# RWKV scan: the mask of the next subchunk taken earlier, the block substitution moved ahead of the levels, and its DMAs spread over three queues

## The reference, cut to what matters

```
def step(S, inp):
    r_t, w_t, k_t, v_t, kk_t, b_t = inp
    sa = jnp.einsum('bhij,bhj->bhi', S, -kk_t)
    S = (S * w_t[:, :, None, :] + sa[..., None] * b_t[:, :, None, :]
         + v_t[..., None] * k_t[:, :, None, :])
    return S, jnp.einsum('bhij,bhj->bhi', S, r_t)
...
y = (rwkv7_scan(r_h, heads(decay[:, :, 0]), k_h, v_h, kk, b_h, False)
     + rwkv7_scan(r_h, heads(decay[:, :, 1]), k_h, v_h, kk, b_h, True))
```

## Time and profile before

| | |
|---|---|
| median of 3 runs | 3489.02 us |
| the profiled execution | 3487.46 us |
| its span | 3486.2 us |
| the scan in the span | about 700 to 1083 us |
| start of one transposed copy to the next, 14 of them from 748.12 to 1061.85 us | 22.4 us mean |
| PE busy in such a stretch | 19.5 us without `cum`, 21.2 to 21.5 us with it |
| DVE busy in such a stretch | about 18.4 us |
| granted TensorE clock in the steady scan | 1.00 |

### The profile page before, as it was taken

One profiled execution on the slowest core, in us unless ns is written; L12 is line 12 of the kernel. 1 busy time (PEld: TensorE's weight loads), 2 busy tenths in 40 slices (PEclk: granted clock), 3 DMA queues, 4 the chain that ended last, 5 costly groups with the idle time before them and its releaser, 6 DMA issues.

```text
span 3486.2 us, 58522 instructions
## 1 busy us (share of the span) xinstructions
PE 3188.2 (91%) x25755; PEld 2622.4 (75%) x25755; DVE 2211.3 (63%) x2948; ACT 971.9 (28%) x1514; POOL 469.5 (13%) x373
## 2 busy tenths in 40 slices
PE   6988788979987999999999897998998799999996
PEld 4777767778885878888888676875667688888885
DVE  5758655778887444444444575997556566666666
ACT  4544233312113221111111444112663111111112
POOL 2530023423224000000000121000001011111110
PEclk9979788989998999999999998999999899999999
DMA  4410044322224011111111202114001111111111
GB/s 131 122 66 14 16 142 138 111 45 42 37 36 166 19 55 51 40 55 53 38 55 43 91 31 74 49 43 99 2 2 61 43 49 49 49 49 49 49 49 67
DMA packets 242726, 207.27 MB, mean 59 GB/s; under 512 B 66744, under 2 KB 205255, under 8 KB 241959
## 3 DMA queue, kind: packets, MB, share of 16 engines
q1 hardware_dynamic: 223527, 176.82, 17.1%
q10 hardware_dynamic: 13824, 25.17, 2.2%
q0 software_dynamic: 5120, 1.53, 0.5%
HBM read 171.93 MB, written 29.64 MB: 58 GB/s over the span
## 4 chain that ended last, share of the span: by engine, by line
PE 70%; DVE 17%; ACT 5%; POOL 2%; issue 2%; DMA 2%; SPq 1%; ACTq 0%; DVEq 0%; POOLq 0%
PE ps L2169 23%; PE ps L2184 17%; PE ps L2031 5%; PE ps L636 3%; PE ps L637 3%; PE ps L638 3%; DVE Yc L2794 2%; DVE s_tmp L1662 2%; DVE s_Z L1663 2%; PE ps L2893 2%; PE ps L2921 1%; PE ps L2911 1%; PE ps L1480 1%; POOL a_x L2544 1%; PE ps L1008 1%
## 5 line engine op out<-in xcount | busy, mean ns | idle before, releaser
L3198 DVE TENSOR_TENSOR H<-H,ps 128x1024 f32<-128x1024 f32 x256 | 312.7, 1221 | 181.6 <-PE ps L2184 174.8
L2334 DVE TENSOR_TENSOR fsum<-fsum,ps 128x1024 f32<-128x1024 f32 x168 | 205.2, 1221 | 312.4 <-PE ps L2184 310.3
L2184 PE MATMUL ps<-dh,hh 128*128 128x512 f32 x864 | 340.0, 393 | 19.9 <-DVE hl L2149 13.9
L2184 PE MATMUL ps<-dl,hh 128*128 128x512 f32 x864 | 338.7, 392 | 0.0
L2184 PE MATMUL ps<-dh,hl 128*128 128x512 f32 x864 | 338.6, 392 | 0.0
L2169 PE MATMUL ps<-hn_h,uh 128*128 128x512 f32 x704 | 275.8, 392 | 7.2 <-DVE ul L1779 4.7
L2169 PE MATMUL ps<-hn_l,uh 128*128 128x512 f32 x704 | 275.4, 391 | 0.0
L2169 PE MATMUL ps<-hn_h,ul 128*128 128x512 f32 x704 | 275.3, 391 | 0.0
L2169 PE MATMUL ps<-hx_h,uh 128*128 128x512 f32 x512 | 200.9, 392 | 8.4 <-DVE hx_l L2149 5.3
L2184 PEld LDWEIGHTS ps<-dh,hh 128*128 128x128 f32 x864 | 163.8, 190 | 58.0 <-DVE hl L2149 15.6
L2169 PE MATMUL ps<-hx_l,uh 128*128 128x512 f32 x512 | 200.4, 391 | 0.0
(11 more groups left out here) (473 smaller groups left out, 7345.8 us busy)
## 6 DMA issues: line engine op xcount, KB each, us to landing
aw<-in_w_ada_dram ACTq DMA_DIRECT2D x96, 256.0 KB, 2.9
uw<-in_w_mlp_dram SPq DMA_DIRECT2D x32, 512.0 KB, 4.3
dw<-in_w_mlp_dram SPq DMA_DIRECT2D x32, 512.0 KB, 5.2
uw<-in_ffn_gate_dram SPq DMA_DIRECT2D x22, 512.0 KB, 4.0
uw<-in_ffn_up_dram SPq DMA_DIRECT2D x22, 512.0 KB, 5.3
dw<-in_ffn_down_dram SPq DMA_DIRECT2D x22, 512.0 KB, 5.9
cw<-in_w_in_dram SPq DMA_DIRECT2D x20, 512.0 KB, 3.8
o_w<-in_w_out_dram SPq DMA_DIRECT2D x16, 512.0 KB, 9.9
```

What stands on the lines that cost most here:

```text
L2184: mm = pe.e.matmul(ps[:, 2 * pair + hf, :], v[s][:, blk(t)], w[:, half(hf)], start=(m == 0), stop=(m == 2))
L2334: return dve.c.tensor_tensor(f, f, new, ALU.add) if g else dve.c.tensor_copy(f, new)
L3198: return dve.c.tensor_tensor(h, h, self.ps[:, 4 + 2 * (t % 2):6 + 2 * (t % 2), :], ALU.add)
```

## The change

The mask `nm` of subchunk n + 1 is taken at the end of pass u, one pass earlier than before, right after `xt`. `s_N16` and `s_Z16` exist twice, and the transposed copy has a tile of its own, `s_X16`. The substitution's steps 0 to 8 now stand ahead of `t4`, its steps 9 to 14 behind the early mask. `products(u + 3)` is cut in three: the first part stands between `t4` and `zz`, the other two between `t5` and `xt`; `pr` is still on the last. The 16 block loads go over three queues: SP 8, ACT 4, POOL 4. The write to `zd` is two DMAs, both issued by ACT, one for each copy. The identity is copied into `s_Z16` by ACT instead of POOL. ACT's exponentials stand in the following odd pass instead of at the end of the even one.

```diff
 SP, for each n:
-            if n:
-                sp.wait_ge(self.t_z["out", n - 1], self.pool["zero"])
-                self.inverse_back(sp, self.t_z, n - 1, range(0, 8, 2))
-            sp.wait_ge(self.t_n["out", n])
-            self.blocks_there(sp, self.t_n, n, range(0, 5))
+            sp.wait_ge(self.t_no["out", n])
+            self.blocks_there(sp, self.t_n, n, range(0, 4))
+            if n:
+                back(n - 1)
...
-            sp.wait_ge(dve["x16", n])
-            sp.e.dma_start(zd[n % 2]..., self.Z16[:]...).then_inc(*self.t_z.one("out", n))
 ACT:
+            if u % 2 and (u + 3) // 2 < NBLK:
+                self.exps_act((u + 3) // 2)
+            if u >= 0:
+                if u + 2 < NSUB:
+                    act.wait_ge(self.t_zo["out", u])
+                    act.e.activation(self.Z16[u % 2][:], self.eye16[:], ACTF.Copy).then_inc(*act.one("one", u + 2))
                 for d in range(2):
                     act.wait_ge(pe["uu", u, d])
                     act.e.activation(self.U[:, L[d]], self.hb(d, 2, 256), ACTF.Copy).then_inc(*act.one("U", u, d))
+            if 0 <= u + 1 < NSUB:
+                act.wait_ge(self.t_no["out", u + 2] if u + 2 < NSUB else dve["z16", u + 1])
+                if u + 2 < NSUB:
+                    self.blocks_there(act, self.t_na, u + 2, range(4, 6))
+                act.wait_ge(dve["z16", u + 1])
+                act.e.dma_start(zd[1], self.Z16[(u + 1) % 2]...).then_inc(*self.t_zo.one())
+                act.wait_ge(dve["x16", u + 1])
+                act.e.dma_start(zd[0], self.X16...).then_inc(*self.t_zo.one("out", u + 1))
 POOL, for each n:
+            if n < NSUB:
+                pool.wait_ge(self.t_no["out", n])
+                self.blocks_there(pool, self.t_nb, n, range(6, 8))
             if n:
                 ...
                 self.inverse_back(pool, self.t_zb, n - 1, range(1, 8, 2))
-            if n < NSUB:
-                pool.e.tensor_copy(self.Z16[:, :, 1], self.eye16[:]).then_inc(*pool.one("one", n))
-                pool.wait_ge(self.t_n["out", n])
-                self.blocks_there(pool, self.t_nb, n, range(5, 8))
 DVE, pass u:
             if n < NSUB:
-                for w, to, name in ((0, self.NM[n % 3], "nm"), (1, self.MM[n % 3], "mm")):
-                    ...
+                masked(1, n)
...
-            if u + 3 < NSUB:
-                products(u + 3)
+            if n < NSUB:
+                self.substitute_dve(n, 0, 9)
             (t4)
+            if u + 3 < NSUB:
+                products(u + 3, 0)
             (zz, t5)
-            if n < NSUB:
-                self.substitute_dve(n, 0, 4)
+            if u + 3 < NSUB:
+                products(u + 3, 1)
+            if u + 3 < NSUB:
+                products(u + 3, 2)
             (xt)
+            if n + 1 < NSUB:
+                masked(0, n + 1)
             if n < NSUB:
-                self.substitute_dve(n, 4, 15)
+                self.substitute_dve(n, 9, 15)
```

More of the change, by code:

```diff
@@ L412, in plan_block1 @@
         self.room = self.r0 + 184 * 1024
-        self.BKT, self.ZZ2, self.Z16 = [sb("s_BKT", [PART, LANES, 2, CH]) for k in range(3)], sb("s_ZZ2", [PART, LANES, 2, CH]), sb("s_Z16", [32, 2, 2, 16, 16])
+        self.BKT, self.ZZ2, self.Z16 = [sb("s_BKT", [PART, LANES, 2, CH]) for k in range(3)], sb("s_ZZ2", [PART, LANES, 2, CH]), [sb("s_Z16", [32, 2, 16, 16]) for k in range(2)]
         self.room = self.r0 + 16 * 1024
@@ L1441, in sig, with back @@
             sp.e.dma_start(self.sig[:], sg[:, t].rearrange("d p c -> p d c")).then_inc(*self.t_in.one("sig", t))
+        def back(n):
+            sp.wait_ge(self.t_zo["out", n], self.pool["zero"])
+            self.inverse_back(sp, self.t_z, n, range(0, 8, 2))
         sig(1)
@@ L1606, in rwkv_scan_act @@
         L = [slice(0, 4), slice(4, 8)]
+        act.wait_ge(self.t_misc["r_const"])
+        for n in range(2):
+            act.e.activation(self.Z16[n][:], self.eye16[:], ACTF.Copy).then_inc(*act.one("one", n))
         for u in range(-2, NSUB):
@@ L1614, in rwkv_scan_act @@
                     act.e.activation(self.U[:, L[d]], self.hb(d, 2, 256), ACTF.Copy).then_inc(*act.one("U", u, d))
+            if 0 <= u + 1 < NSUB:
+                zd = self.dram["zd"][(u + 1) % 2].rearrange("k x d w i c -> w (k x) d (i c)")
+                act.wait_ge(self.t_no["out", u + 2] if u + 2 < NSUB else dve["z16", u + 1])
+                if u + 2 < NSUB:
+                    self.blocks_there(act, self.t_na, u + 2, range(4, 6))
+                act.wait_ge(dve["z16", u + 1])
+                act.e.dma_start(zd[1], self.Z16[(u + 1) % 2][:].rearrange("p d i c -> p d (i c)")).then_inc(*self.t_zo.one())
+                act.wait_ge(dve["x16", u + 1])
+                act.e.dma_start(zd[0], self.X16[:].rearrange("p d i c -> p d (i c)")).then_inc(*self.t_zo.one("out", u + 1))
+            elif u == -2:
+                act.wait_ge(self.t_no["out", 0])
+                self.blocks_there(act, self.t_na, 0, range(4, 6))
             if 0 <= u < NSUB // 2:
@@ L1662, in substitute_dve @@
             dve.c.tensor_tensor(part, col, pivot, ALU.mult).then_inc(*dve.one())
-            dve.c.tensor_tensor(rows, rows, part, ALU.subtract).then_inc(*dve.one())
+            dve.c.tensor_tensor(rows, rows, part, ALU.subtract).then_inc(*(dve.one("z16", n) if s == 14 else dve.one()))
         if end == 15:
-            dve.c.tensor_copy(self.Z16[:, :, 0], self.Z16[:, :, 1].rearrange("p d i c -> p d c i")).then_inc(*dve.one("x16", n))
+            if n:
+                dve.wait_ge(self.t_zo["out", n - 1])
+            dve.c.tensor_copy(self.X16[:], self.Z16[n % 2][:].rearrange("p d i c -> p d c i")).then_inc(*dve.one("x16", n))
     def rwkv_scan_dve(self):
@@ L1677, in both, with products @@
             return bass.AP(tensor=x.tensor, offset=x.offset, ap=[x.ap[0], [y.offset - x.offset, 2]] + list(x.ap[1:]))
-        def products(n):
+        def products(n, part):
             t, AR, BK, F = n // 2, self.AR[n % 3], self.BK, self.F[n % 3]
@@ L1699, in products @@
[L1699 to L1704, removed]
+            if part == 0:
+                dve.wait_ge(act["Ei", t, 0], act["Ei", t, 1])
+                if n >= 3:
+                    dve.wait_ge(pe["yy", n - 3, 1])
+                if n:
+                    dve.wait_ge(pe["tr", n - 1, 1])
+                dve.c.tensor_tensor(lanes(F[:]), lanes(self.last[:]), end, ALU.mult).then_inc(*dve.one())
+                dve.e.tensor_tensor(lanes(AR[:, :, 0]), both(self.kk[:, :, W], self.kk[:, :, W_b]), Ex, ALU.mult).then_inc(*dve.one())
+            elif part == 1:
+                dve.e.tensor_tensor(lanes(BK[:, :, 0]), both(self.bb[:, :, W], self.bb[:, :, W_b]), En, ALU.mult).then_inc(*dve.one())
+                dve.e.tensor_tensor(lanes(AR[:, :, 1]), both(rkv[:, 0:4, W], rkv[:, 0:4, W_b]), Ei, ALU.mult).then_inc(*dve.one())
+            else:
+                dve.e.tensor_tensor(lanes(BK[:, :, 1]), both(rkv[:, 4:8, W], rkv[:, 4:8, W_b]), En, ALU.mult).then_inc(*dve.one())
+                dve.c.tensor_copy(lanes(self.last[:]), end).then_inc(*dve.one("pr", n))
@@ new lines, in masked @@
+        def masked(w, n):
+            to, name = ((self.NM[n % 3], "nm"), (self.MM[n % 3], "mm"))[w]
+            for d in range(2):
+                dve.wait_ge(pe[("gb", "gk")[w], n, d])
+                dve.e.tensor_tensor(to[:, L[d]].rearrange("p l a b -> p l (a b)"), self.fb(d, w),
+                                    rep(self.gram_mask[:, d].rearrange("p a b -> p (a b)"), 4), ALU.mult).then_inc(*dve.one(name, n, d))
+        for part in range(3):
+            products(0, part)
+        masked(0, 0)
```

33 lines of the change are left out of this document (12 added, 21 removed).

## The result

| | before | after |
|---|---|---|
| median of 10 runs, us | 3489.4 | 3501.4 |
| lowest to highest | 3484.5 to 3499.8 | 3495.1 to 3511.2 |
| ratio after to before | | 1.0037 (95%: 1.0022 to 1.0052) |
| the profiled execution | 3487.5 | 3511.2 |

The changed kernel is slower by 12 us; 3497 was forecast. The profiled execution of the changed kernel happens to be its slowest. So I profiled both kernels twice (experiments 1 and 9) and read the scan by its own marks: start is from the first AR product to the first `t4`, steady from there to the fifteenth `t4`, end from there to the last one.

The account below looks back on a forecast made before the run. Two loops of nearly equal length bound the scan: DVE and DRAM 22.4 us, PE alone 22.1. Terms +1.2 +4.2 +6.8 -4.1 = +8.1 on 3487.5 give 3495.6, plus 1.6 for the median: 3497; own range 3492 to 3501, whole 3484 to 3508.

Parts of the forecast that it names:

- the waits that it named: In the scan: PE idle about 1.6 us ahead of the grams, DVE 1 to 2 us for block loads, none for `nm`.
- Products behind `t5`: DVE's products after `t5` delay the next grams from 0.57 to 2.15 us; PE stands 1.6 us longer in 14 full periods.
- The blocks over three queues: Blocks reach DVE 8.0 us after the mask, DVE waits 1.6; second `zd` write 1.0 us after the copy.
- The copy without POOL: With the identity copy on ACT, the product that took 1.02 us beside POOL's copy takes 0.6.
- The sum of a period: Eight full periods without `cum` take 22.55 us (+0.15 each), six with `cum` 23.1 (+0.7 each).
- The levels: The stretch from `t4` to the end of the second `t5`: 4.5 us in every period.
- The start: Scan's start: uncovered `products(1)` and slow first grams put the first `t4` at 741.3 against 734.49, +6.8 us.
- The end: Pass 13 has no further products, gram or mask; `t4` comes 13.0 us after `t5` instead of 17.1, -4.1 us.
- The first rival: Load paths are shorter than read and PE alone decides the period: not slower, 3485.5 us; chance 0.18.
- The second rival: Queues get in each other's way, so blocks or ZZ come 1 us later: +10 us, 3507; chance 0.25.
- The rule beside it: GpSimd can't write descriptors during a DVE copy within SBUF: blocks 0.6 us later in 8 periods, sum 3502.

Follow-up runs that it names:

- experiment 1: The changed kernel run again unaltered, with a second profile: median 3505.7 us, ratio 1.0033 to the kernel before.
- experiment 9: The kernel before run again unaltered, for a second profile: median 3495.5 us, ratio 0.9998, steady part 321.0 us.
- Experiment 3: Changed kernel, but the grams `gb` wait for the third product instead of the mark `pr` behind the fourth: 3491.7 us, ratio 0.9994 to the kernel before.
- experiment 7: Changed kernel, but block loads read the previous subchunk's buffer and don't wait for the write (result wrong): 3496.8 us, ratio 1.0003 to the kernel before.
- experiment 8: Changed kernel, but block loads over two queues, ten on SP and six on POOL, none on ACT: 3523.7 us, ratio 1.0074 to the kernel before.
- experiment 2: Changed kernel, but `products(1)` stands ahead of the substitution of subchunk 0: 3499.6 us, ratio 1.0007 to the kernel before.
- experiment 4: Changed kernel, but the 512 KB `sig` load waits for `t5` of the subchunk whose ZZ was loaded: 3503.8 us, ratio 1.0023 to the kernel before.
- experiment 10: Changed kernel with `products(1)` early, `gb` waiting for the third product, and 8 double-size block loads instead of 16: 3480.5 us, ratio 0.9950 to the kernel before.
- experiment 11: Changed kernel with `products(1)` early, AR products before the substitution, first BK product between `t4` and `zz`, 8 double block loads: 3480.8 us, ratio 0.9959 to before.

## Why the prediction was right or wrong

The sign held, and so did the waits that it named. The median of 3501.4 lies just above the forecast's own range (3492 to 3501) and inside the whole one (3484 to 3508). The likeliest class did not hold: 0.52 stood on no measurable change, 0.36 on slower, and it is slower. By its own steps:

*Products behind `t5`*: right. PE's grams start 2.07 after `t5` (2.15 forecast), after 1.33 of idle. Experiment 3 takes 0.8 of it away and gets 0.8 in the quiet periods with `cum` and 0.4 to 0.9 in those without. Those without `cum` gain too, because the mask, the write and the block loads hang on the grams as well. That was in my own chain; the sum's wording put the cost on PE's periods alone.

*The blocks over three queues*: the path was 7.5 where read (8.0), and it does end periods, by experiments 7 and 8. That ACT's place in it costs the `zd` write 0.9 us is seen (1.0 forecast).

*The copy without POOL*: right. The products take 0.60 each, the 1.02 of the earlier trace rows is gone.

*The sum of a period* failed in its size, in both directions. Quiet periods are shorter than forecast, 22.7 and 21.8 to 22.2 against 23.1 and 22.55. But each of the two profiles has seven of 23.3 to 24.9. Without the levels the forecast's periods sum to 256.0 (6 x 18.6 and 8 x 18.05), and 257.7 and 255.4 were measured: right in the sum, by short and long ones that cancel. I had summed fixed durations. Four things in a row now have no slack behind them: the write to `nd`, the block loads, the write to `zd`, the ZZ loads. Any one that is late adds its lateness.

*The levels* are the term that was mis-sized. I took 4.5 us for them in every period. In the changed kernel they took 5.4 to 6.2 in five and in three of the 14 periods of the two profiles, and in one of the two ends, at a granted clock below 0.8. Against the kernel before that is +3.1 in the steady part and +0.7 in the end, together as much as the 3.6 between the forecast's 8.1 and the 11.7 measured. 1.6 of it, in both profiles, is the first stretch of levels, right behind the 9 us for which PE stands at the start. In the full periods the slow ones follow waits of PE of 1.5 to 3.8 us, but waits of 1.2 to 2.0 were followed by no slow one in the first profile of the kernel before, and one of 2.8 by none in the second of the changed kernel; so how long PE stood doesn't alone decide it, and the cause stays open. The kernel before has it as well: I took one profile of it as its fixed time, and only experiment 9 showed its steady part to be 3.6 below the mean of two.

*The start*: +6.8 as forecast, and experiment 2 shows that the products and the grams behind them are the cause. To the tenth it is luck. The slow first grams are there (3.32 us for 32), but steps 0 to 8 ended 39.4 after the first products instead of 41.0, and the first `t4` then waited 2.2 us, which the forecast did not have, for the ZZ load behind the sig load (experiment 4).

*The end*: -3.0 where -4.1 was forecast. The second profile's 17.8 us is as forecast (17.6); in the first (19.4) the levels ahead of the last copy took 5.9 us instead of 4.5, with a granted clock of 0.79 from 1074 to 1082.

*The first rival* (PE alone decides) is out. Waits of DVE for blocks run through all profiles of the changed kernel. *The second rival* has its part in single periods, by late ZZ loads and by POOL's late start; its sum of +10 on top of the forecast is not there.

*The rule beside it.* The rule of the Trainium skill (SBUF — State Buffer, section "SBUF: two separate sides") would have POOL's issues stretched by the copy of 0.6 us that now falls among them. The traces agree, but only where the copy hits the beginning of an issue:
```profile
806.29 2.87 POOL L1426 DMA_DIRECT2D s_N<-nd_dram  x4 [15.06 <-DMA nd_dram<-s_NM]
806.57 0.59 DVE L1686 COPY s_X<-s_Z 32x512 f32<-32x512 f32 x1
...
876.88 2.48 POOL L1426 DMA_DIRECT2D s_N<-nd_dram  x4 [15.50 <-DMA nd_dram<-s_NM]
877.28 0.59 DVE L1686 COPY s_X<-s_Z 32x512 f32<-32x512 f32 x1
```
In the first pass the copy began 0.28 us after POOL's first issue, and that issue took 1.02 instead of 0.62; in the second it began 0.40 after, and none was longer. Over the eleven profiles of the changed kernel and of its variants every block load's issue that the copy met from 0.1 before to 0.28 after its start took 0.69 us or more and ended 0.15 us (0.26 in experiments 10 and 11) behind the copy; every one that it met from 0.30 on kept its time. In the changed kernel that is three passes of 14 in one profile and one in the other, 0.1 to 0.4 us each, instead of 0.6 in 8 periods.

What stays open: why POOL starts its block loads 1.4 us later at subchunks 8 and 15, what makes the granted clock fall in one pass and not in another, and why the last ZZ load lands some 1 us late in some passes in which no sig load is near.

## What to carry to other kernels

Before work is moved to "behind" a step, look at which mark sits on its last instruction and who waits for that mark: here three products with the mark on the small copy behind the last cost PE 1.3 us in every pass, and moving the mark alone won as much as the whole change lost. In a pipelined loop a prologue pass runs the same code without the cover that the steady passes have, so it is to be priced by itself. And a loop whose slack has been taken out pays for every late DMA: compare such versions with two profiles each, inside the stage, and against the spread of the kernel before. Sum apart the stretches of fixed work whose length hangs on the clock: without the levels, the profiles of the changed kernel and of experiments 2 and 4 agree within 3 us, with them only within 5.

## What the runs showed of the hardware

The issue of a small DMA cost by the piece hardly at all: 0.62 us for 64 pieces of 64 bytes on POOL, 0.70 for 128; 0.37 per load on ACT and SP. A POOL issue whose beginning a DVE copy within SBUF met took up to 1.03 us instead of 0.62 and ended 0.15 us behind the copy. A ZZ load of 16 KB that POOL issued 0.12 to 0.26 us behind SP's sig load of 512 KB took 4.0 to 5.2 us to land in most cases, and 2.0 where the sig load came later. A POOL copy beside a DVE product with both inputs in SBUF lengthened the product from 0.60 to 1.02 us, and the product is back at 0.60 with the copy on ACT. After PE had waited some 3.8 us its granted clock was 0.75 over the next 6 us, and the levels took 5.4 us for 4.5; the same work took 6.2 at 0.61 to 0.66. The part of this kernel ahead of the scan varies by 12 us between profiles, as much as the whole effect.
